# Two transformer blocks on one core: input sums on VectorE, modulation pairs in other places, gates head by head, one weight sum on GpSimd

## The chip, the cores and the metric

The kernel runs on one core of a Trainium2 chip. The time is that of the device, from the first to the last instruction and what lies around them, in microseconds (us). Lower is better. TensorE (PE) multiplies matrices, VectorE (DVE) and ScalarE (ACT) work on elements of SBUF and PSUM, GpSimd (POOL) works on SBUF alone, and SyncE (SP) issues the weight loads.

## The reference, cut to what matters

Two layers in a row on `x` of 512 tokens by 1024 features, all in fp32. The first has a gated spatial unit, forgetting attention and a SwiGLU feed-forward part:

```python
merged = jax.nn.sigmoid(g_a) * y_a + jax.nn.sigmoid(g_b) * y_b     # y_b: attention, y_a: spatial gating
x = x + rmsnorm(merged @ w_out[l], mix_post_g[l])
h = rmsnorm(x, ffn_pre_g[l])
x = x + rmsnorm(swiglu(h, w_gate[l], w_up[l], w_down[l]), ffn_post_g[l])
```

The second is a hybrid layer (short convolution, stick-breaking attention, a state-space mixer) whose norms are modulated by a vector `c`:

```python
mod = jax.nn.silu(c) @ mod_w + mod_b             # 1024 by 6144
shift1, scale1, gate1, shift2, scale2, gate2 = jnp.split(mod, 6, axis=-1)
h = rms_norm(x, g_pre_mix) * (1 + scale1) + shift1
merged = (sigmoid(gl_a) * y_a + sigmoid(gl_b) * y_b + sigmoid(gl_c) * y_c)
x = x + gate1 * rms_norm(merged @ w_o, g_post_mix)
h2 = rms_norm(x, g_pre_ffn) * (1 + scale2) + shift2
gt, up = jnp.split(h2 @ w_ffn_in, 2, axis=-1)
x = x + gate2 * rms_norm((silu(gt) * up) @ w_ffn_out, g_post_ffn)
```

## The kernel before

Every engine runs one program written out by hand, and the engines meet at semaphores; each engine works strictly in its own order. Every fp32 matrix product is made of three matmuls over a high and a low part of each operand: ACT casts a weight unit to its high part (`w_hi`, L1100), DVE subtracts to get the low part (`w_lo`, L1585, "split"), and PE multiplies high by high, high by low and low by high (L2295 to L2297). A weight unit is 1 MB, loaded by SP into one of two `raw` slots; a slot is free when the low part of the unit before in it is done.

**Seven-product units.** The up stage of both layers (`hidden` on DVE and ACT, `blocks` on POOL and PE) has 22 units. The first four (`tile`, `split`) are plain. The other 18 (`BLOCKS`) are multiplied as two-by-two blocks with seven products of 12 matmuls each instead of eight (`product`, L2389 to L2391, 256 columns), in the order p7 m, p6 m, p4 m, p1 m+1, p5 m, p2 m+1, p3 m. For this the inputs need four sums S1 to S4 of quarters of `h` (in `s_sum`, `s_hi`, `s_lo`), made once for each layer, and the weights four sums for each unit: t1 (DVE, L1729), t3 (DVE, L1735), t2 (POOL, L993), and t4 = t2 minus a quarter (POOL, L997). DVE then makes low parts: of the pair of raw quarters (`pair_lo`, L1742), of t3 and t2 (`sums_lo`, L1751, which waits for t4, since it overwrites what t4 reads), of t4 and t1 (L1758) and of the last quarter (`b22_lo`, L1765). DVE also adds the products: p2 (L1803), z (L1813), c21 (L1818), c22 (L1824), the gate multiplications (L1829, L1797). PE may begin p3 of a unit only when c22 of that unit is there. A step of this loop is called a turn here.

**The sums of the inputs.** At the start of the stage DVE makes S1 (L1770 to L1772) ahead of the first `tile`, POOL makes S3, S2 and S4 (L977 to L985).

**The modulation.** POOL makes `mod` in six pairs of 512 columns each times two: `mod_begin(pair)` clears `mod_acc` (L944), loads the bias and the first slab; `mod_step(pair, i)`, i = 0 to 15, issues the load of the next slab (L939, 256 KB), multiplies a slab by a scalar in each partition (L957) and adds it (L960). The 16th step raises `mod_summed`. A pair cannot begin before PE has read the one before (`mod_read`). Pairs 0 to 3 are turned to columns by eight transposes on PE (`mod_columns(pair)`, L2566), which wait for `mod_summed` of the pair, and summed by DVE (`mod_columns(pair, ...)`, L1700). Pairs 4 and 5 are gates (`mod_gate`, L2574). Pair 1 scales the norm ahead of the mixer of the second layer, pairs 2 (shift) and 3 (scale) belong to the norm ahead of its second feed-forward part.

| POOL makes | before | after |
|---|---|---|
| pair 0 | at the start | same |
| pair 1, steps | 8 before the layer norm's roots, 5 after, 3 in `blocks` of layer 1 | 9 before, 4 after, 3 in `blocks` (one each in turns 1 to 3) |
| pair 2 | `blocks` of layer 1, one step a turn | whole, in the down stage of layer 1 |
| pair 3 | whole, in the down stage of layer 1 | begins after the squares of the mixer's output in layer 2; two steps before `rr_ssm` (L1071), 14 after |
| pair 4 | after `rr_ssm` | after pair 3 |
| pair 5 | `blocks` of layer 2, one step a turn | 4 steps ahead of post-norm 2, 12 in `blocks` (turns 1 to 12) |

**The end of the mixer in layer 2.** PE runs gate unit n_mg, then the sums of squares (L2871), gate unit n_mg+1, the spread of the roots (L2877, which waits for DVE's `rr_diag`, which waits for POOL's `rr_ssm`), gate unit n_mg+2, then the branches' unit n_mg+3. A gate unit is 48 matmuls of 512 columns. After that come twelve more units, the output product `out2` (in it `mod_gate(4)`), post-norm 2 and the up stage of layer 2.

**The gates of the heads.** After the attention's last mask POOL adds 1 to the eight gate tiles (L1021), then multiplies the eight heads by them (L1024), then begins pair 1. The layer norm of the spatial unit needs POOL's roots (`ln_root`, L1031, L1032), which come after 8 steps of pair 1; DVE normalizes with them (L1945) and PE goes on with L2660.

Of the kernel before, what the change touches and what calls it, by code (L numbers as in the profile page):

```python
# [31 lines left out]
F32 = mybir.dt.float32  # L32
# [9 lines left out]
KD = D // P  # L42
# [101 lines left out]
def build(nc, a, out):  # L144
    with ExitStack() as ctx:
# [509 lines left out]
        def dve_order():  # L655


            yield from ("s1", "s1_lo", "s3_lo", "s24_lo", "t1 0", "t3 0", "pair 0", "sums 0", "t4 0", "t1_lo 0")
            for m in range(BLOCKS):
# [5 lines left out]
                yield from [f"t3 {ahead}"] if ahead else []  # L665
# [6 lines left out]
        def act_order():  # L672

            yield from ("s1_hi", "s3_hi", "s24_hi", "pair 0", "sums 0", "p1 0", "t4 0", "t1 0")
# [19 lines left out]
        def wait_pool(eng, which, m, total):  # L694


            eng.wait_ge(block_pool, (2 * BLOCKS + 3) * which + 2 * m + 3 + total)

        def wait_pool_sum(eng, which, done):


            eng.wait_ge(block_pool, (2 * BLOCKS + 3) * which + done)
# [178 lines left out]
        def _(gp):  # L881
# [91 lines left out]
            def blocks(n0, which, c):  # L973

                s1, s2, s4, s3 = (s_sum[:, i] for i in (S1, S2, S4, S3))
# [6 lines left out]
                wait_pool_sum(gp, which, 2)  # L982
                then(gp.tensor_tensor(s2, s2, h_quarter(h_lo, 0, 0), ALU.subtract))
                then(gp.tensor_tensor(s4, h_quarter(h_hi, 0, 1), s2, ALU.subtract))
                gp.tensor_tensor(s4, s4, h_quarter(h_lo, 0, 1), ALU.add).then_inc(block_pool, 1)  # L985
                if which == 0:
                    mod_step(1, 13)
                for m in range(BLOCKS):
                    n = n0 + PLAIN + m
                    t2, t4 = four(operand(w_sum, n0, 3)), four(t4_sum(n0, m))  # L990
# [1929 lines left out]
```

## Time and profile before

| | |
|---|---|
| median of 3 runs | 1578.08 us (1577.12 to 1578.24) |
| profiled execution, its own time | 1577.7 us |
| its span | 1576.0 us |
| granted TensorE clock, mean | 0.993 |
| busy: PE, DVE, POOL, ACT | 1533.7, 1018.0, 687.7, 669.8 us |
| idle of PE by waits | 35.6 us in 38 waits |

A busy PE is the sum over pipelined matmuls, so the waits of PE say more than its share. In a row of the timeline the text in brackets is how long the engine sat idle before the instruction, and what ended that.

### The profile page before, as it was taken

Reading aid. Unit: us, or ns where it says so; the run is one execution under the profiler, and the core shown is the slowest. Engines: PE = TensorE matmul, PEld = TensorE weight load, DVE = VectorE, ACT = ScalarE, POOL = GpSimd, SP = SyncE. Lnnn points to the kernel's source line nnn. Section 1 sums busy time; section 2 is a strip of 40 time slices with the busy share of each in tenths; the row PEclk is TensorE's granted clock in tenths of the full one; section 3 lists DMA queues with packets and bytes.
Section 4 is the critical chain, followed back from the end, with each engine's and each line's share of the span. In section 5 each row is a group of like instructions: output and inputs, shape, how many; then the busy total and the mean of one; then the engine's idle time right before and its main releaser. Section 6 shows DMA issues by size and latency. Waiting matters only on the chain.

```text
span 1576.0 us, 23248 instructions
## 1 busy us (share of the span) xinstructions
PE 1533.7 (97%) x8908; PEld 1346.1 (85%) x8908; DVE 1018.0 (65%) x1379; ACT 669.8 (43%) x1109; POOL 687.7 (44%) x543
## 2 busy tenths in 40 slices
PE   9999999979989999999999999999999899999998
PEld 9878788868889999988898888888889799999886
DVE  4342766447588999964276979643457799997423
ACT  6223444313454444442176775323236344544221
POOL 3871002760776656669120802691003666662000
PEclk9999999989999999999999999999999999999999
DMA  7532132422523434454322212443322243444231
GB/s 216 174 120 80 54 81 55 147 87 80 182 73 101 132 104 133 128 181 146 115 67 81 81 54 69 139 141 106 106 80 81 60 131 113 126 134 134 95 107 54
DMA packets 189620, 171.40 MB, mean 109 GB/s; under 512 B 20688, under 2 KB 162000, under 8 KB 189520
## 3 DMA queue, kind: packets, MB, share of 16 engines
q1 hardware_dynamic: 181456, 144.84, 30.6%
q0 software_dynamic: 8064, 25.20, 5.2%
q8 instruction: 67, 1.10, 0.3%
q14 instruction: 33, 0.27, 0.1%
HBM read 167.91 MB, written 2.10 MB: 108 GB/s over the span
## 4 chain that ended last, share of the span: by engine, by line
PE 70%; DVE 15%; POOL 9%; issue 4%; ACT 1%; DMA 0%; DVEq 0%; POOLq 0%; ACTq 0%
PE bank L2295 17%; PE bank L2297 17%; PE bank L2296 17%; POOL w_sum L997 3%; DVE w_lo L1751 3%; DVE act_m L1829 3%; POOL w_sum L993 2%; DVE w_lo L1742 2%; PE bank L2458 2%; PE bank L2459 2%; PE bank L2462 2%; DVE w_lo L1758 2%; DVE act_m L1729 1%; PE bank L2389 1%; PE bank L2616 1%
## 5 line engine op out<-in xcount | busy, mean ns | idle before, releaser
L1585 DVE TENSOR_TENSOR w_lo<-raw,w_hi 128x2048 fp32r<-128x2048 f32 (+1 forms) x109 | 216.3, 1985 | 239.4 <-ACT w_hi L1100 239.3
L2295 PE MATMUL bank<-h_hi,w_hi 128*128 128x512 f32 (+1 forms) x800 | 310.9, 389 | 11.1 <-DVE w_lo L1585 11.1
L2297 PE MATMUL bank<-h_hi,w_lo 128*128 128x512 f32 (+1 forms) x800 | 299.8, 375 | 0.0
L2296 PE MATMUL bank<-h_lo,w_hi 128*128 128x512 f32 (+1 forms) x800 | 299.6, 375 | 0.0
L1100 ACT CAST w_hi<-raw 128x2048 fp32r<-128x2048 f32 (+1 forms) x108 | 171.4, 1587 | 199.4 <-PE bank L2297 191.8
L957 POOL TENSOR_SCALAR mod_raw<-mod_raw,c_silu 128x512 f32<-128x512 f32 x96 | 197.0, 2053 | 19.3 <-DMA mod_raw<-in_mod_w 15.6
L2295 PEld LDWEIGHTS bank<-h_hi,w_hi 128*128 128x128 f32 x800 | 151.9, 190 | 40.0 <-DVE w_lo L1585 12.4
L2389 PE MATMUL bank<-s_hi,w_hi 128*128 128x256 f32 x576 | 166.7, 289 | 13.4 <-DVE act_m L1824 13.4
L2296 PEld LDWEIGHTS bank<-h_lo,w_hi 128*128 128x128 f32 x800 | 152.0, 190 | 27.4 <-issue 1.9
L2297 PEld LDWEIGHTS bank<-h_hi,w_lo 128*128 128x128 f32 x800 | 151.6, 189 | 27.7
L2391 PE MATMUL bank<-s_hi,w_lo 128*128 128x256 f32 x576 | 162.9, 283 | 0.0
L2390 PE MATMUL bank<-s_lo,w_hi 128*128 128x256 f32 x576 | 162.9, 283 | 0.0
L960 POOL TENSOR_TENSOR mod_acc<-mod_acc,mod_raw 128x512 f32<-128x512 f32 x96 | 138.1, 1438 | 8.3
L2389 PEld LDWEIGHTS bank<-s_hi,w_hi 128*128 128x128 f32 x576 | 110.2, 191 | 20.0 <-DVE act_m L1824 19.9
L2389 PE MATMUL bank<-h_hi,w_hi 128*128 128x256 f32 x432 | 122.4, 283 | 0.0
L2390 PE MATMUL bank<-h_lo,w_hi 128*128 128x256 f32 x432 | 122.2, 283 | 0.0
L2391 PE MATMUL bank<-h_hi,w_lo 128*128 128x256 f32 x432 | 122.1, 283 | 0.0
L2390 PEld LDWEIGHTS bank<-s_lo,w_hi 128*128 128x128 f32 x576 | 110.3, 192 | 0.0
L2391 PEld LDWEIGHTS bank<-s_hi,w_lo 128*128 128x128 f32 x576 | 110.3, 192 | 0.0
L2295 PE MATMUL bank<-w_hi,act_hi 128*128 128x512 f32 x280 | 109.0, 389 | 0.0
L2297 PE MATMUL bank<-w_hi,act_lo 128*128 128x512 f32 x280 | 108.9, 389 | 0.0
L2296 PE MATMUL bank<-w_lo,act_hi 128*128 128x512 f32 x280 | 108.9, 389 | 0.0
(476 smaller groups left out, 3348.3 us busy)
## 6 DMA issues: line engine op xcount, KB each, us to landing
raw<-in_w_in SPq DMA_DIRECT2D x102, 512.0 KB, 4.5
mod_raw<-in_mod_w POOLq DMA_DIRECT2D x96, 256.0 KB, 3.0
raw<-in_w_ffn_in SPq DMA_DIRECT2D x44, 512.0 KB, 4.9
raw<-in_w_gate SPq DMA_DIRECT2D x22, 512.0 KB, 4.0
raw<-in_w_up SPq DMA_DIRECT2D x22, 512.0 KB, 5.3
raw<-in_w_down SPq DMA_DIRECT2D x20, 512.0 KB, 4.5
raw<-in_w_ffn_out SPq DMA_DIRECT2D x20, 512.0 KB, 4.5
raw<-in_w_out SPq DMA_DIRECT2D x8, 512.0 KB, 4.3
```

The source lines that it names most:

```text
L957: then(gp.tensor_scalar(mod_raw[:, s, :], mod_raw[:, s, :], c_silu[:, k:k + 1], None, ALU.mult))
L960: ins = gp.tensor_tensor(acc, acc, mod_raw[:, s, :], ALU.add)
L997: gp.tensor_tensor(t4, t2, quarter_of(n, 1, 0), ALU.subtract).then_inc(block_pool, 1)
L1100: ins = act.copy(w_hi[s][:, cols], raw[s][:, cols])
L1585: ins = dve.tensor_tensor(w_lo[s][:, cols], raw[s][:, cols], w_hi[s][:, cols].bitcast(F32), ALU.subtract)
L1751: dve.tensor_tensor(operand_pair(w_lo, n0, 2), operand_pair(w_sum, n0, 2), operand_pair(w_hi, n0, 2).bitcast(F32), ALU.subtract).then_inc( ...
L2295: pe.matmul(o, st_hi, mv_hi, start=first, stop=False)
L2296: pe.matmul(o, st_hi, mv_lo, start=False, stop=False)
L2297: return pe.matmul(o, st_lo, mv_hi, start=False, stop=last)
L2389: pe.matmul(o, hi[:, k, :], mv_hi(k), start=first and k == 0, stop=False, skip_group_check=not first)
L2390: pe.matmul(o, hi[:, k, :], mv_lo(k), start=False, stop=False, skip_group_check=not first)
L2391: ins = pe.matmul(o, lo[:, k, :], mv_hi(k), start=False, stop=k == 3, skip_group_check=not first)
```

## The change

The input sums S1, S2 and S4 are all made by DVE, later than before (S1 after the first tile and the first split, S2 and S4 after t1 of block 0); POOL makes S3 alone, and waits ahead of its last part for the low part of unit 2. t3 is made by POOL, ahead of t2, instead of DVE. The pairs of the modulation move as in the table above; PE's transposes of pair 1 go to the last block of layer 1, those of pair 2 to the down stage, and those of pair 3 stand ahead of the branches' first unit, where PE waits for `mod_summed` of that pair; DVE's sums of the columns move with them. The low and high parts of hidden tiles 4 and 5 move from turn 8 to the first unit of the down stage. The gates are added to and applied head by head in one loop.

```diff
             def blocks(...)        # POOL
-                wait_dve(gp, which, "s1")
-                gp.tensor_tensor(s2, s1, h_quarter(h_hi, 0, 0), ALU.subtract).then_inc(block_pool, 1)
-                then(gp.tensor_tensor(s2, s2, h_quarter(h_lo, 0, 0), ALU.subtract))
-                then(gp.tensor_tensor(s4, h_quarter(h_hi, 0, 1), s2, ALU.subtract))
-                gp.tensor_tensor(s4, s4, h_quarter(h_lo, 0, 1), ALU.add).then_inc(block_pool, 1)
+                gp.wait_ge(lo_done, n0 + 3)      # ahead of the last part of s3
                 for m in range(BLOCKS):
+                    wait_operand_free(gp, n0, which, m, 2)
+                    gp.tensor_tensor(t3, quarter_of(n, 1, 1), quarter_of(n, 0, 1), ALU.subtract).then_inc(block_pool, 1)
                     wait_dve(gp, which, f"t1 {m}")
...
-                    if which == 0:
-                        if m == 0:
-                            mod_step(1, 14)
-                            mod_step(1, 15)
-                        elif m == 1:
-                            mod_begin(2)
-                        else:
-                            mod_step(2, m - 2)
-                    elif m == 0:
-                        mod_begin(5)
-                    elif m <= 2 * KD:
-                        mod_step(5, m - 1)
+                    if 1 <= m <= 2 * KD - done:
+                        mod_step(pair, done + m - 1)
...
             for f in range(KD):
                 wait_emptied(gp, n_g + 4 + f // 2, f % 2)
                 then(gp.tensor_scalar(gates[:, KD + f, :], gates[:, KD + f, :], 1.0, None, ALU.add))
-            for f in range(KD):
                 gp.wait_ge(head_out, f + 1)
                 gp.tensor_tensor(q_t[:, f, :], q_t[:, f, :], gates[:, KD + f, :], ALU.mult).then_inc(gated_b, 1)
             mod_begin(1)
-            for i in range(8):
+            for i in range(9):
                 mod_step(1, i)
...
-            blocks(n_up, 0, 1)
-            mod_pair(3)
+            blocks(n_up, 0, 1, 1, 13)
+            mod_pair(2)
...
+            mod_begin(3)
+            for i in range(2):
+                mod_step(3, i)
             gp.wait_ge(ms2_ready, 1)
             gp.tensor_tensor(rr_ssm[:], ms_ssm[:], ...).then_inc(rr_ready, 1)
+            for i in range(2, 2 * KD):
+                mod_step(3, i)
             mod_pair(4)
             mod_lo_part(4)
+            mod_begin(5)
+            for i in range(4):
+                mod_step(5, i)
             post_norm(2)
-            blocks(n_up2, 1, 3)
+            blocks(n_up2, 1, 3, 5, 4)
...
             # DVE, start of hidden
+                tile(n0, 0, 0)
+                split(n0 + 2)
                 dve.wait_ge(h_lo_done, 2 * KD * (c + 1))
                 then(dve.tensor_tensor(s1, h_quarter(h_hi, 1, 0), h_quarter(h_hi, 1, 1), ALU.add))
...
+                then(dve.tensor_tensor(s2, s1, h_quarter(h_hi, 0, 0), ALU.subtract))
+                then(dve.tensor_tensor(s2, s2, h_quarter(h_lo, 0, 0), ALU.subtract))
+                then(dve.tensor_tensor(s4, h_quarter(h_hi, 0, 1), s2, ALU.subtract))
+                dve.tensor_tensor(s4, s4, h_quarter(h_lo, 0, 1), ALU.add).then_inc(block_dve, 1)
...
             # DVE, in a turn
-                    if m + 1 < BLOCKS:
-                        t3_part(m + 1)
-                    if m == 2 and which == 0:
-                        mod_columns(1, gain_3, True)
-                    if m == 8:
-                        hidden_lo(which, PLAIN)
-                        hidden_lo(which, PLAIN + 1)
...
             # PE
             pe.wait_ge(ssm_lo_done, 4)
-            pe.wait_ge(mod_out, 4)
-            branches(n_mg + 3, STILL)
+            mod_columns(3)
+            branches(n_mg + 3, STILL, 4)
```

## Rows read from the trace of the kernel before

**Rows 1.** Waits of PE: engine, line, releaser: us in total, times, longest.

```profile
PE bank L2389 <- DVE act_m L1824: 13.4, 32, 1.3
PE bank L2295 <- DVE w_lo L1585: 11.1, 2, 6.6
PE bank L2660 <- DVE v_sgu L1945: 9.0, 1, 9.0
```

**Rows 2.** Chain that ended last, by time (start us, us, what), PE at the mixer's end.

```profile
1000.42 1.78 PE bank L2877 x16
1002.20 0.23 PE bank L2295
```

**Rows 3.** Timeline of ACT: start us, us, line, operation; idle before in brackets.

```profile
1013.14 0.60 ACT L1190 ACTIVATE sig<-bank 128x512 f32<-128x512 f32 x1 [3.94 <-PE bank L2297]
```

**Rows 4.** Timeline of POOL from the squares on, pair 4's first steps and fifteenth.

```profile
979.37 3.21 POOL L1069 TENSOR_TENSOR z_t<-z_t 128x512 f32<-128x512 f32 x1
990.92 1.68 POOL L1071 TENSOR_TENSOR rr_ssm<-ms_ssm,power 128x8 f32<-128x8 f32 x1 [8.34 <-DVE ms_ssm L2238]
992.55 0.96 POOL L944 MEMSET mod_acc<- 128x1024 f32 x1
...
1000.31 1.57 POOL L957 TENSOR_SCALAR mod_raw<-mod_raw,c_silu 128x512 f32<-128x512 f32 x1 [4.30 <-DMA mod_raw<-in_mod_w]
1004.19 2.65 POOL L957 TENSOR_SCALAR mod_raw<-mod_raw,c_silu 128x512 f32<-128x512 f32 x1
...
1058.29 1.58 POOL L957 TENSOR_SCALAR mod_raw<-mod_raw,c_silu 128x512 f32<-128x512 f32 x1
```

**Rows 5.** Timeline of DVE, the diagonals of the roots.

```profile
994.09 1.65 DVE L2242 TENSOR_SCALAR rr_diag<-ident,rr_ssm 128x128 f32<-128x128 f32 x8
```

**Rows 6.** Stretches around PE's longest wait; the column after POOL is the granted clock.

```profile
340.00:345.00 5.00, 0.00 (x1) 0.00 (x1) 3.25 (x4) 0.00 (x0) 3.58 (x7) 0.50 0.00 0
345.00:350.00 5.00, 5.00 (x22) 4.72 (x23) 2.68 (x4) 0.00 (x0) 0.00 (x0) 0.60 0.00 0
```

**Rows 7.** Timelines, POOL's heads' gates and pair 1, then DVE's layer norm.

```profile
284.35 14.14 POOL L1024 TENSOR_TENSOR q_t<-q_t,gate_a 128x512 f32<-128x512 f32 x8
304.18 1.57 POOL L957 TENSOR_SCALAR mod_raw<-mod_raw,c_silu 128x512 f32<-128x512 f32 x1 [2.33 <-DMA mod_raw<-in_mod_w]
...
286.14 0.69 DVE L1898 COPY q_t<-bank 128x512 f32<-128x512 f32 x1 [3.30 <-PE bank L2639]
340.07 0.81 DVE L1945 TENSOR_SCALAR v_sgu<-v_sgu,mean_var,inv_rms 128x1024 f32<-128x1024 f32 x1 [9.74 <-POOL inv_rms L1032]
```

**Rows 8.** Timeline of POOL and DVE in one turn.

```profile
557.11 1.29 POOL L993 TENSOR_TENSOR w_sum<-raw,act_m 128x512 f32<-128x512 f32 x1 [3.42 <-DVE act_m L1729]
557.24 1.72 DVE L1735 TENSOR_TENSOR w_sum<-raw 128x512 f32<-128x512 f32 x1
558.55 1.56 POOL L997 TENSOR_TENSOR w_sum<-w_sum,raw 128x512 f32<-128x512 f32 x1
```

**Rows 9.** Chain that ended last, in turns with a step and around turns 2 and 8.

```profile
520.75 1.21 DVE mod_sum L1700 x2
...
552.53 1.44 DVE act_m L1829
...
563.14 1.43 DVE act_m L1829
...
585.79 1.21 DVE act_lo L1710 x2
```

**Rows 10.** Timeline of DVE, start of the up stage in layer 1.

```profile
457.79 3.67 DVE L1585 TENSOR_TENSOR w_lo<-raw,w_hi 128x2048 fp32r<-128x2048 f32 x1 [1.11 <-ACT w_hi L1100]
496.72 0.42 DVE L1824 TENSOR_TENSOR act_m<-bank,act_m 128x256 f32<-128x256 f32 x1
```

**Rows 11.** Timeline of POOL at post-norm 2; and PE's gate product, first and last start.

```profile
1186.19 0.32 POOL L894 TENSOR_SCALAR sq_y<-sq_y 128x1 f32<-128x1 f32 x1 [23.77 <-ACT y_out L1106]
L2574 PE MATMUL bank<-mod_lo,ones_r x4: 389/389/389, 1165.5 to 1487.4; 128*128 128x512 f32 x4
```

More of the change, by code:

```diff
@@ L655, in dve_order @@
         def dve_order():
-            yield from ("s1", "s1_lo", "s3_lo", "s24_lo", "t1 0", "t3 0", "pair 0", "sums 0", "t4 0", "t1_lo 0")
+            yield from ("s1", "s3_lo", "t1 0", "s24", "s1_lo", "pair 0", "s24_lo", "sums 0", "t4 0", "t1_lo 0")
             for m in range(BLOCKS):
@@ L672, in act_order @@
         def act_order():
-            yield from ("s1_hi", "s3_hi", "s24_hi", "pair 0", "sums 0", "p1 0", "t4 0", "t1 0")
+            yield from ("s3_hi", "s1_hi", "pair 0", "s24_hi", "sums 0", "p1 0", "t4 0", "t1 0")
             for m in range(BLOCKS):
@@ L694, in wait_pool @@
         def wait_pool(eng, which, m, total):
-            eng.wait_ge(block_pool, (2 * BLOCKS + 3) * which + 2 * m + 3 + total)
-        def wait_pool_sum(eng, which, done):
-            eng.wait_ge(block_pool, (2 * BLOCKS + 3) * which + done)
+            eng.wait_ge(block_pool, (3 * BLOCKS + 1) * which + 3 * m + 1 + total)
         POST_UNIT = [n_out + 3, n_dn + 11, n_out2 + 3, n_dn2 + 11]
@@ L971, in mod_pair, with blocks @@
                     mod_step(pair, i)
-            def blocks(n0, which, c):
-                s1, s2, s4, s3 = (s_sum[:, i] for i in (S1, S2, S4, S3))
+            def blocks(n0, which, c, pair, done):
+                s3 = s_sum[:, S3]
                 gp.wait_ge(h_lo_done, 2 * KD * (c + 1))
@@ L1033, in _ @@
             gp.wait_ge(merged, KD)
-            for i in range(8, 13):
+            for i in range(9, 13):
                 mod_step(1, i)
             post_norm(0)
-            blocks(n_up, 0, 1)
-            mod_pair(3)
+            blocks(n_up, 0, 1, 1, 13)
+            mod_pair(2)
             post_norm(1)
@@ L1144, in post_norm @@
                 for j in range(units):
-                    if units == 6 and 1 <= j <= 4:
-                        for t in range(4 * j + 2, 4 * j + 6):
+                    if units == 6 and j <= 4:
+                        for t in range(4 if j == 0 else 4 * j + 2, 4 * j + 6):
                             hidden_hi(k // 2, t)
@@ L1225, in t4_t1_hi @@
                 def t4_t1_hi(m):
-                    wait_pool(act, which, m, 2)
+                    wait_pool(act, which, m, 3)
                     wait_operand_free(act, n0, which, m, 4)
@@ L1638, in post_norm @@
                 for j in range(units):
-                    if units == 6 and 1 <= j <= 4:
-                        for t in range(4 * j + 2, 4 * j + 6):
+                    if units == 6 and j <= 4:
+                        for t in range(4 if j == 0 else 4 * j + 2, 4 * j + 6):
                             hidden_lo(k // 2, t)
@@ L1784, in hidden @@
                                   ALU.subtract).then_inc(block_dve, 1)
-                t1_part(0)
-                tile(n0 + 2, 2, 0)
-                t3_part(0)
-                pair_lo(0)
                 sums_lo(0)
@@ L2437, in blocks @@
                     product(m, 6, "x", *sums(S4), first=False)
-                    if m == 0 and which == 0:
-                        mod_columns(1)
             def token_unit(n, x_hi, x_lo, k0, first, last, pace, width=512, tiles=range(NT)):
@@ L2848, in gate_unit, with branches @@
                     feature_tile(n, f, pace)
-            def branches(n, pace):
+            def branches(n, pace, columns=0):
                 u = UNITS[n]
@@ L2857, in branches @@
                     wait(pe, emptied[2 + f], u["round"] + pace.by(pace.rounds))
+                    if f == 1:
+                        wait(pe, mod_out, columns)
                     for b, k0, x_hi, x_lo, kt in ((4 + 2 * f, 2, sb_hi, sb_lo, 2), (5 + 2 * f, 4, ssm_hi, ssm_lo, 4), (2 + f, 0, sc_hi, sc_lo, 2)):
```

62 lines of the change are left out of this document (25 added, 37 removed).

## The prediction

> **What bounds the kernel now.** I read the waits of PE first. There are only three that matter [rows 1]: 13.4 us before p3 of 32 turns, on c22 of DVE; 11.1 us in two waits for a low part, at the start of the two up stages; 9.0 us for the layer norm of the spatial unit. Elsewhere PE never stops for long, so a change pays only by shortening these three, and it costs wherever it makes PE stop anew. Then I read the timelines of POOL and DVE around each place that the change touches, to see how much earlier than PE's need each moved piece is ready.
>
> **Part 1, pair 3 moved to the end of the mixer.** This is the largest term. PE spreads the roots at 1000.42 and starts gate unit n_mg+2 at 1002.20 [rows 2]. ACT takes that unit's second tile at 1013.14 [rows 3], so PE is at the branches' unit n_mg+3 at 1013.1. In the new program it first has to transpose pair 3 there, and for that POOL must have done all 16 steps.
>
> When can POOL have done them? The squares end at 979.37 + 3.21 = 982.6 [rows 4]. The moved `mod_begin` issues three loads after its memset; for pair 4 the first multiplication came 1000.31 - 992.55 = 7.8 us after the memset [rows 4], so for pair 3 it starts at about 990.4, or some 2 us sooner if the first slab lands sooner. A step is 3.88 us at best (1004.19 - 1000.31) and 4.14 us on the mean of fourteen (1058.29 - 1000.31 = 57.98), which ran beside DVE's work [rows 4]. The two steps ahead of `rr_ssm` take 7.8 to 8.3 us, to 996.2 to 998.7. Only then does POOL make `rr_ssm`, which it did at 990.92 before, after an idle time of 8.34 us. It ends at about 998.5 (997 to 1000), and DVE's diagonals (1.65 us, [rows 5]) end at 1000.2 instead of 995.7. PE wants them at 1000.42: the cover of nearly 5 us is used up, and I take 0 to 1.5 us of wait, 0.5 in the sum.
>
> Fourteen steps are left. At 3.88 they are 54.3 us, at 4.14 58.0. DVE has little to do once PE stands, so I take 56.5: the last sum is there at 998.5 + 56.5 = 1055.0. PE stands from 1013.1 to 1055.0, 41.9 us (the 0.5 of above is inside this). Ends: 997 + 54.3 = 1051.3, 38 us; 1000 + 58 + 1 = 1059, 46 us. Nothing covers this wait: on PE's queue all that follows stands behind the transposes, and SP's loads, ACT and DVE wait for PE in turn. The eight transposes themselves only change place.
>
> After so long an idle time PE starts slowly. In the one long wait of now the granted clock was 0.50 in the stretch of the wait and 0.60 in the next 5 us [rows 6], that is the lower of the two levels, 1.2 GHz, for four of these five, after which it is at 2.4 GHz. Working through 4 us at half speed costs 2.0 us. Part 1 in all: **+44** (40 to 49).
>
> **Part 2, what stands behind it.** Pair 4 takes POOL 78 us more, to about 1134, while PE, shifted by 44, wants it at 1165.5 + 44 = 1209 [rows 11]: covered by 75 us. Pair 5 begins only when PE has read pair 4, about 1 us after that. Seen in the old times: 1166.5, first step 7.8 us later, four steps to 1190 (1187 at best), where POOL's first root was due at 1186.19 [rows 11]. POOL's root of tile 0 is thus 1 to 4 us late. DVE multiplies a second bank before it uses this root, which covers about 2 us. I take +0.5 (0 to 3).
>
> **Part 3, the gates head by head.** POOL's eight multiplications began at 284.35, when the last gate tile was done, and took 14.14 us [rows 7]. Seven of the heads are there long before; head 7 is copied at 286.14 [rows 7]. One multiplication is left after it: end at about 289.5 instead of 298.5. Pair 1 begins 9 us earlier, and has 9 steps instead of 8 before the roots, one more of about 4.2 us. The roots come 4.8 us earlier. They are what DVE's normalization waited 9.74 us for [rows 7], and PE's wait of 9.0 us hangs on that. The gain is 4.8 (2 to 8), and with the shorter idle time perhaps a little of the slow clock: **-5**. The seven multiplications now lie beside the attention, whose DVE steps mostly read PSUM; I take nothing for that, and 1 us if they get in its way.
>
> **Part 4, the start of the up stages.** PE waits 11.1 us in two waits [rows 1] for the split that stands behind S1 on DVE (457.79, 3.67 us, [rows 10]). With the tile and split first, the split neither waits for S1 nor runs beside a sum of POOL, and PE's wait nearly goes. But DVE has not less to do in the stage's start: it gains three sums of 1.1 us, each beside POOL's t3, t2 and t4. Laying out DVE's new order by its durations, I come to the first c22 at about 496, where it was at 496.72 [rows 10]; PE meets the wait later, in small pieces. So I take **-2** for both stages (0 from the layout, up to -10 if all of PE's earlier start is kept, +2 if POOL's t3 delays S2 and S4 more).
>
> **Part 5, the turns.** A turn with a step of the modulation takes 563.14 - 552.53 = 10.61 us [rows 9]. PE has 84 matmuls in it, which is 10.1 us when the mean wait of 13.4/32 = 0.42 [rows 1] and 0.1 for starting again are taken off. The loop that sets the 10.61 runs over DVE and POOL: pair_lo, b22_lo, t1, then POOL's t2 and t4, then sums_lo, c22, the low parts of t4 and t1, the gate. Three edits change it:
> - t3 leaves DVE, where it took 1.72 us beside t2 [rows 8], but stood off the loop: DVE waits for t4 after it anyway. t4 becomes 1.29 instead of 1.56 [rows 8], and starts a little sooner: -0.33.
> - t3 on POOL (about 1.29, as t2 in [rows 8]) can start only after p7, which is about when DVE ends pair_lo. Then it holds up b22_lo, and with it t1 and t2: +0.8.
> - Without a step of the modulation, DVE's gate multiplication (1.44 us in [rows 9]) is 0.41, and t1's low part is freer: -1.25.
>
> A turn with a step becomes 10.61 - 0.33 + 0.8 = 11.1, a turn without one 10.61 - 0.33 - 1.25 + 0.8 = 9.8 by DVE and POOL. Then PE's own loop counts (p3, p7, t3, b22_lo, t1, t2, t4, sums_lo, c22), which I add up to 10.25, so it is 10.25 (10.08 to 10.4). Layer 1 has 3 turns with a step and 13 without: 3 x 0.5 - 13 x 0.35 = -3.1, and turns 2 and 8 lose their extra 1.21 us each [rows 9], -2.4; in all -5.5. Layer 2 has 12 with and 4 without: 12 x 0.5 - 4 x 0.35 = +4.6, less 1.2 of turn 8: +3.4. Together **-2** (-9 to +6). The columns' sums and the tiles 4 and 5 moved to the down stage stand there ahead of splits that PE needs over 1 us later: nothing.
>
> *A rule weighed.* DVE's t3 starts at 557.24 and ends 0.56 us after POOL's t2 (558.40), so it waited for it and needs 0.56 us itself [rows 8]. If every such pair shut each other out, a turn could not be shorter than the sum: on DVE 4.8 us (two of 1024 columns, four of 512, one of 256, at 0.56 for 512), on POOL 6.7 us in a turn with a step (four of 1.29, one of 1.57 [rows 4]), together 11.5 instead of my 11.1. The same sum for the kernel of now, with t3 on DVE, is 10.8, where 10.61 is measured [rows 9]. The Trainium skill states this exclusion (SBUF — State Buffer, section "SBUF: two separate sides"): the pair of ports goes to whichever of the two engines starts first, for the whole instruction. The rows of t3 agree, the length of a turn does not quite; by the rule 15 turns would cost 6 us more.
>
> **Sum.** 44 + 0.5 - 5 - 2 - 2 = +35.5 to the profiled execution's 1577.7 us gives 1613.2; that execution stands 0.4 us under the median, so the runs' median should be **1614** us.
>
> **Rivals.**
> - *The stall does not come* (PE's need for pair 3 is covered after all). Then 1577.7 - 8.5 = 1569. It decides at one point: the 16 steps would have to be over by 1013.1. For it speaks only that the mixer's part has idle time of POOL (8.34 us before `rr_ssm`). Against it: 14 steps at 3.88 us after 998. It is faster than before: chance 0.03. If POOL's steps ran in half the time, the stall would be 15 us and the result 1587: 0.04.
> - *The stall comes, and the other parts give more*: PE keeps its earlier start in both up stages, all turns without a step run at 10.1, and the roots come 8 us earlier: -8 - 4 - 3 further, 1600. Chance 0.13.
> - *The stall is longer and t3 hurts more*: steps at 4.14 us throughout and the first slab late, +4, the up stages give nothing, +2, the turns with a step take 11.4, +4.5: 10.5 more, 1624. Chance 0.13.
> - *Full exclusion in the turns with a step*: 15 turns at 11.5 instead of 11.1, +6, 1620. For it speaks t3's row, against it that it gives 10.8 for the 10.61 of now. Chance 0.07. The page named above states it.
> - *The forecast*, 1605 to 1622 in all its small terms: chance 0.60.
>
> The range is 1602 to 1624. A measurement of this kernel tells 0.2%, 3.2 us, from no change. Faster by more than that 0.03, the same 0.01, slower 0.96.
>
> **What the profile of the changed kernel would show.** Right: one wait of PE of 38 to 46 us before the transposes of pair 3, released by POOL's last `mod_acc`; a granted clock near 0.5 in it and a little after; 14 steps of 3.9 to 4.1 us in it on POOL; the wait at L2660 near 4 to 5 us; the wait for a low part at the start of the up stages under 1 us each, but others after it; turns of about 10.25 without and 11.1 with a step. Wrong: if pair 3's steps end before PE is there, part 1 falls, and with it the sign. If the turns with a step stay at 10.6, POOL's t3 found a gap that I do not see. If the first c22 of the stage comes at 491 instead of 496, part 4 was too small by 5 us for each stage.

## The result, and the profile after

The changed kernel takes 1613.73 us (median of 4 runs, 1611.45 to 1614.3) where the kernel before, timed beside it, takes 1577.63 us: a ratio of 1.0226, 95% interval 1.0208 to 1.0244. The profiled execution took 1614.3 us, its span 1612.6 us, 36.6 more than the 1576.0 of before. The forecast was 1614.

The waits of PE in the changed kernel (columns as in [rows 1]):

```profile
PE bank L2535 <- POOL mod_acc L954: 37.6, 1, 37.6
PE bank L2362 <- DVE act_m L1801: 13.0, 20, 1.1
PE bank L2629 <- DVE v_sgu L1916: 6.6, 1, 6.6
PE bank L2362 <- DVE w_lo L1718: 3.4, 2, 1.7
PE bank L2848 <- DVE rr_diag L2214: 3.1, 1, 3.1
```

One row is new and longer than all waits of before together (35.6 us): the transposes of pair 3 (L2535) stand 37.6 us for POOL's last `mod_acc`. The 11.1 us for the low part at the start of the up stages ([rows 1], second row) are gone, the spatial unit waits 6.6 instead of 9.0 us, and the diagonals of `rr_ssm`, which cost PE nothing before, 3.1 us.

The same place on POOL, from the first step of pair 3 on, and on PE (timelines):

```profile
979.34 2.27 POOL L951 TENSOR_SCALAR mod_raw<-mod_raw,c_silu 128x512 f32<-128x512 f32 x1 [3.19 <-DMA mod_raw<-in_mod_w]
981.70 1.28 POOL L954 TENSOR_TENSOR mod_acc<-mod_acc,mod_raw 128x512 f32<-128x512 f32 x1
983.28 0.58 POOL L933 DMA_DIRECT2D mod_raw<-in_mod_w  x1 [0.30 <-POOL mod_acc L954]
983.90 2.66 POOL L951 TENSOR_SCALAR mod_raw<-mod_raw,c_silu 128x512 f32<-128x512 f32 x1
...
988.01 1.68 POOL L1053 TENSOR_TENSOR rr_ssm<-ms_ssm,power 128x8 f32<-128x8 f32 x1
989.66 0.63 POOL L933 DMA_DIRECT2D mod_raw<-in_mod_w  x1
990.33 1.67 POOL L951 TENSOR_SCALAR mod_raw<-mod_raw,c_silu 128x512 f32<-128x512 f32 x1
...
1044.44 1.26 POOL L954 TENSOR_TENSOR mod_acc<-mod_acc,mod_raw 128x512 f32<-128x512 f32 x1
1045.85 1.51 PE L2535 MATMUL bank<-ident,mod_acc 128*128 128x128 f32 x6 [37.58 <-POOL mod_acc L954]
```

POOL has no gap over 0.30 us between 988.01 and 1045.70: `rr_ssm`, then fourteen steps in 56.0 us (989.66 to 1045.70), 4.0 each. PE starts 0.15 us after the last of them.

The windows around the end of that wait (columns as in [rows 6]; the granted clock stands after POOL):

```profile
1008.00:1045.00 37.00, 0.27 (x2) 0.00 (x0) 2.29 (x1) 2.38 (x2) 33.33 (x28) 0.54 0.32 92
1045.00:1050.00 5.00, 4.15 (x14) 3.70 (x15) 1.45 (x3) 0.00 (x0) 2.50 (x4) 0.50 0.00 0
1050.00:1055.00 5.00, 5.00 (x19) 4.00 (x19) 0.00 (x0) 0.00 (x0) 2.81 (x4) 0.82 0.34 106
1055.00:1060.00 5.00, 5.00 (x24) 4.13 (x23) 3.44 (x5) 0.62 (x1) 4.49 (x5) 1.00 0.20 52
```

PE works from 1045.85 on, at 0.50 (1.2 GHz) until nearly 1052, then at 2.4 GHz.

**Where the 36.6 us arose.** I took the start of the same instruction in both traces and subtracted (after minus before, running total):

| place | before | after | total | own share |
|---|---|---|---|---|
| PE, spatial unit (L2660, L2629) | 345.00 | 343.07 | -1.9 | gates, -1.9 |
| PE, second transposes of the norm ahead of the up stage, layer 1 | 441.76 | 440.55 | -1.2 | within what single runs differ by |
| DVE, first c22, layer 1 | 496.72 | 494.04 | -2.7 | start of the stage, -1.5 |
| DVE, c22 of turn 16, layer 1 | 669.05 | 659.20 | -9.8 | turns, -7.2 |
| PE, transposes behind the down stage | 796.33 | 786.48 | -9.8 | 0 |
| DVE, first merge after the mixer | 1018.68 | 1055.31 | +36.6 | pair 3, +46.5 |
| PE, second transposes of post-norm 2 | 1210.16 | 1247.31 | +37.1 | +0.5 |
| DVE, first c22, layer 2 | 1267.70 | 1300.82 | +33.1 | start of the stage, -4.0 |
| DVE, c22 of turn 16, layer 2 | 1438.52 | 1475.12 | +36.6 | turns, +3.5 |

Between the first two rows the total changes by +0.7: the stretch takes 97.48 us at a mean granted clock of 0.97, where it took 96.76 at 0.98 (windows 343.07:440.55 and 345.00:441.76). The first row belongs to this one execution of the changed kernel. Eight of the experiments below (e1 to e4, e7 to e10) run the same program up to there, and PE waits 4.7 to 4.9 us in them, not 6.6; part 3 below comes back to this.

### The profile page after: what moved, and what is told of

It is laid out like the page before. It is cut to its first block, busy times and chain, and to the rows that moved or that the text cites. A ratio compares the mean times of both kernels' runs of the same rounds, so it can differ in the third digit from the quotient of the medians.

```text
span 1612.6 us, 23286 instructions
## 1 busy us (share of the span) xinstructions
PE 1535.8 (95%) x8908; PEld 1347.0 (84%) x8908; DVE 970.4 (60%) x1351; ACT 669.0 (41%) x1109; POOL 710.6 (44%) x571
## 4 chain that ended last, share of the span: by engine, by line
PE 71%; DVE 11%; POOL 11%; issue 4%; ACT 2%; DMA 1%; DVEq 0%; SPq 0%; POOLq 0%; ACTq 0%
PE bank L2268 15%; PE bank L2270 15%; PE bank L2269 15%; PE bank L2362 4%; PE bank L2364 4%; PE bank L2363 4%; POOL mod_raw L951 3%; POOL mod_acc L954 2%; PE bank L2430 2%; PE bank L2429 2%; PE bank L2433 2%; DVE w_lo L1727 2%; POOL w_sum L987 1%; POOL w_sum L983 1%; DVE w_lo L1718 1%
## 5 line engine op out<-in xcount | busy, mean ns | idle before, releaser
L1568 DVE TENSOR_TENSOR w_lo<-raw,w_hi 128x2048 fp32r<-128x2048 f32 (+1 forms) x109 | 212.6, 1951 | 231.9 <-ACT w_hi L1087 231.7
L951 POOL TENSOR_SCALAR mod_raw<-mod_raw,c_silu 128x512 f32<-128x512 f32 x96 | 192.2, 2002 | 22.8 <-DMA mod_raw<-in_mod_w 19.0
L980 POOL TENSOR_TENSOR w_sum<-raw 128x512 f32<-128x512 f32 x36 | 64.8, 1800 | 141.1 <-PE bank L2364 125.2
```

What stands on the lines that cost most here:

```text
L951: then(gp.tensor_scalar(mod_raw[:, s, :], mod_raw[:, s, :], c_silu[:, k:k + 1], None, ALU.mult))
L980: gp.tensor_tensor(t3, quarter_of(n, 1, 1), quarter_of(n, 0, 1), ALU.subtract).then_inc(block_pool, 1)
L1568: ins = dve.tensor_tensor(w_lo[s][:, cols], raw[s][:, cols], w_hi[s][:, cols].bitcast(F32), ALU.subtract)
```

## The experiments

All twelve were timed beside the kernel before; the ratio is to that one, and where two experiments come from different series they are compared by their ratios.

**e1_two_steps and e2_eight_steps: is it the wait?** Steps of pair 3 left out behind `rr_ssm` (the loads of their slabs go with them).

```diff
-            for i in range(2, 2 * KD):
+            for i in (14, 15):                       # e1
+            for i in (2, 3, 4, 5, 6, 7, 14, 15):     # e2
                 mod_step(3, i)
```

> Left out: 12 of the 14 steps of pair 3 that stand behind rr_ssm (steps 2 to 13), so the sum of this pair is incomplete. Theory (the added time is the time that PE stands before the transposes of pair 3): the two steps that stay behind the root end at about 993 + 8 = 1001, PE is there only at about 1010, so its wait of 37.6 us goes and with it the slow clock after it (2 to 3 us): 1614 - 40 = 1573 to 1574 us. Rival (the pair's work costs by lying beside DVE and PE, or the rest of the change costs, and PE's wait would be filled by another): the time stays over 1590 us, with a new wait of PE in the trace after 1010.

> Left out: steps 8 to 13 of pair 3, so the sum of this pair is incomplete; eight of the fourteen steps behind rr_ssm stay. Theory (PE's wait is the time of the steps, one for one, and the slow clock behind it is a fixed sum): a step is 4.0 us, six fewer take 24 us off the wait of 37.6, which leaves 13.6, with the granted clock still at its lower level behind it: 1590 us. Rival (the wait isn't set by POOL's steps one by one, or the slow clock depends on the length of the wait): off this by more than 3 us.

e1: 1571.24 us, ratio 0.9953 (0.9937 to 0.9968). e2: 1589.14 us, 1.0062 (1.0046 to 1.0078). PE's wait before the transposes is gone in e1; in e2 its timeline has

```profile
1021.59 1.94 PE L2541 MATMUL bank<-ident,mod_acc 128*128 128x128 f32 x8 [14.22 <-POOL mod_acc L960]
```

Six steps fewer shorten the wait by 23.4 us, 3.9 each, and the stretch from the down stage's transposes to the first c22 of layer 2 by 23.9 (the transposes themselves start 22.3 us earlier in it). Without a wait before the transposes (e1) that stretch is 41.0 us shorter than in the changed kernel: 37.6 of wait and 3.4 more, most of which is the low clock behind the wait (last section). The rival (another wait fills the gap) is out: e1 has no new one. It keeps the wait for the diagonals, 2.9 us, and behind it the clock is low as well (a window of e1, columns as in [rows 6]):

```profile
993.00:996.00 3.00, 3.00 (x13) 2.76 (x12) 3.00 (x5) 1.24 (x2) 2.92 (x2) 0.50 0.26 65
```

**e10_rr_first: is the 3.1 us wait for the diagonals a cost of its own?** `mod_begin(3)` stays, the two steps go behind the root.

```diff
             mod_begin(3)
-            for i in range(2):
-                mod_step(3, i)
             gp.wait_ge(ms2_ready, 1)
             gp.tensor_tensor(rr_ssm[:], ...)
...
+            for i in range(2):
+                mod_step(3, i)
             for i in range(2, 2 * KD):
                 mod_step(3, i)
```

> The changed kernel, with the two steps of pair 3 that stood ahead of rr_ssm put behind it. Theory (PE's two waits end in one, the time at which POOL's last step is done): rr_ssm comes about 5 us earlier, so the wait of 3.1 us for the diagonals goes, but POOL stands until 981.1 for its input and then takes 1.7 us for it, so the steps start 3.4 us later and the wait before the transposes grows by 3.1 + 3.4: 1614 + 3.4 = 1617 us. Rival (the 3.1 us wait for the diagonals is a cost of its own): 1611 us.

1613.31 us, ratio 1.0221 (1.0207 to 1.0235): no different from the changed kernel. The waits of PE:

```profile
PE bank L2535 <- POOL mod_acc L954: 43.8, 1, 43.8
PE bank L2362 <- DVE act_m L1801: 13.5, 20, 1.1
PE bank L2629 <- DVE v_sgu L1916: 4.7, 1, 4.7
```

The wait for the diagonals is gone and the one behind it has grown by 6.2 us. The time alone does not tell the two apart: the theory's 1617 us lies outside the interval of the ratio (1610.3 to 1614.7 us over the 1577.63 of the first series), the rival's 1611 just inside. The stretch does: from the down stage's transposes to the first merge behind the mixer it is 269.4 us, against 268.8 in the changed kernel, and the rival wants it 3.1 us shorter. So the 3.1 us cost nothing. Of the 3.4 us that the theory also expected, 1.2 came at the transposes. The steps start 4.1 us later (counted from the down stage's transposes), but `rr_ssm` (1.7 us) no longer stands among them, which the theory left out, and from the first multiplication to the last sum the sixteen steps took 63.4 us (981.88 to 1045.29) against 64.7 in the changed kernel (979.34 to 1045.70, less `rr_ssm`).

**e6_gates_apart and e11_six_before_roots: what do the gates and the ninth step do?**

```diff
             for f in range(KD):                      # e6
                 ...
                 then(gp.tensor_scalar(gates[:, KD + f, :], gates[:, KD + f, :], 1.0, None, ALU.add))
+            for f in range(KD):
                 gp.wait_ge(head_out, f + 1)
...
-            for i in range(9):                       # e11
+            for i in range(6):
                 mod_step(1, i)
             ...                                      # the roots
+            for i in range(6, 9):
+                mod_step(1, i)
             gp.wait_ge(merged, KD)
```

> The nine steps before the roots stay, but POOL adds 1 to all gate tiles first and multiplies only then. Theory: the eight multiplications take 14.1 us from 284.35, as before the change, and end at 298.5 instead of 290.7; all that follows on POOL is 7.8 us later, so PE's wait before the spatial unit grows from 6.6 to 14.4 us: 1614 + 7.8 = 1621 to 1622 us. Rival (the two orders are worth little, since what POOL does in the attention's stretch is slowed there): the time grows by under 3 us.

> The changed kernel with six instead of nine steps of pair 1 ahead of the spatial unit's roots; the other three follow right behind the roots. Theory (the roots wait for POOL's steps, and the gates' 7 to 8 us went into the ninth step and into longer steps): the roots are then bound by DVE's variance at 331, some 6 us earlier, PE's wait of 6.6 us goes and about 1 us of the slow clock behind it: 1606 to 1607 us. Rival (three steps beside DVE's later work make PE wait elsewhere): under 3 us gained.

e6: 1617.47 us, ratio 1.0254 (1.024 to 1.0268), 3.7 us above the changed kernel (4.4 by the ratios), half of what the theory said and more than the rival. POOL's first step starts 7.3 us later (304.37 instead of 297.06), near the 7.8 expected, but the nine steps take 37.1 us instead of 40.2, and PE waits 10.8 instead of 6.6 us:

```profile
PE bank L2630 <- DVE v_sgu L1917: 10.8, 1, 10.8
```

Why nine steps are longer in the changed kernel shows in its own timeline of POOL:

```profile
287.49 3.20 POOL L1003 TENSOR_TENSOR q_t<-q_t,gate_a 128x512 f32<-128x512 f32 x1 [2.78 <-DVE q_t L1869]
297.06 1.64 POOL L951 TENSOR_SCALAR mod_raw<-mod_raw,c_silu 128x512 f32<-128x512 f32 x1 [3.02 <-DMA mod_raw<-in_mod_w]
...
306.52 3.32 POOL L954 TENSOR_TENSOR mod_acc<-mod_acc,mod_raw 128x512 f32<-128x512 f32 x1
...
316.16 1.56 POOL L951 TENSOR_SCALAR mod_raw<-mod_raw,c_silu 128x512 f32<-128x512 f32 x1 [1.58 <-DMA mod_raw<-in_mod_w]
317.80 2.36 POOL L954 TENSOR_TENSOR mod_acc<-mod_acc,mod_raw 128x512 f32<-128x512 f32 x1
```

An addition of 1.29 us takes 3.32 or 2.36 here, beside DVE's splits, and a slab comes 1.6 us late. The late slab is this execution's alone: in the eight kernels with the same program up to there no slab is late, the nine steps take 38.1 to 38.9 us, and PE waits 4.7 to 4.9 us (4.7 in the list of e10 above). Against these e6 makes the wait 6 us longer. e11: 1607.24 us, ratio 1.018 (1.0166 to 1.0193), 6.5 to 7.3 below the changed kernel, as the theory said. PE does not wait for the spatial unit (0.1 us is left), but its timeline a little later has

```profile
353.54 0.50 PE L2270 MATMUL bank<-h_hi,w_hi 128*128 128x512 f32 x1 [2.19 <-DVE w_lo L1570]
```

PE starts the spatial unit 6.5 us earlier than in the changed kernel (336.61 instead of 343.07), and then finds a low part 2.2 us away. The granted clock is 1.00 from there to the norm's transposes, where it was 0.97 over 97 us; the 2.2 us use up most of what this gives back. So the roots were late by POOL's steps alone: they now wait for DVE's variance.

**e3_no_steps_turns, e4_t3_dve and e5_before_t3_pool: what sets a turn?** e3 leaves out steps 4 to 13 of pair 5; e4 gives t3 back to DVE; e5 is the kernel before with t3 on POOL.

```diff
+                    if which == 1 and m in (12, 13):      # e3
+                        mod_step(5, m + 2)
-                    if 1 <= m <= 2 * KD - done:
+                    if which == 0 and 1 <= m <= 2 * KD - done:
                         mod_step(pair, done + m - 1)
...
-                    gp.tensor_tensor(t3, quarter_of(n, 1, 1), quarter_of(n, 0, 1), ...)      # e4; e5 adds it
+                    dve.tensor_tensor(t3, quarter_of(n, 1, 1), quarter_of(n, 0, 1), ...)     # behind z; e5 takes it away
```

> Left out: steps 4 to 13 of pair 5, so the sum of this pair is incomplete; turns 2 to 11 and one more of layer 2's up stage have no step of the modulation, turns 12 and 13 keep one each. Theory (a turn with a step is 11.07 us by the loop over DVE and POOL, a turn without one 10.11 by PE): ten turns fewer with a step give 10 x 0.96 = 9.6 us: 1604 us. Rival (the turns of layer 2 are long for another cause than the steps, such as t3 on POOL by itself): they stay near 11 and the time near 1614.

> t3 is back on VectorE in both layers (ahead of the turn's pair_lo, as before the change), all else as in the changed kernel. Theory (t3 on POOL lengthens the loop over DVE and POOL by holding up b22_lo, and this loop sets only the turns with a step of the modulation): those turns go from 11.07 to 10.6 us, the turns without one stay at 10.1, where PE's own work sets them. Fifteen turns with a step (12 in layer 2, 3 in layer 1): 15 x 0.46 = 6.9 us less, 1607 us. Rival (t3 has no part in the longer turns, the new order on DVE has): 1614 us.

> The kernel before with t3 moved to POOL and nothing else. Theory: its 30 turns with a step go from 10.61 to 11.07 us, since POOL's t3 comes ahead of t2 and holds up b22_lo: 30 x 0.46 = 13.8 us more, 1591 to 1592 us. Rival (t3 costs the same on either engine, and the 11.07 come from another part of the change): 1578 us.

e3: 1602.53 us, ratio 1.0154 (1.0139 to 1.017). e4: 1602.74 us, 1.0148 (1.0132 to 1.0163). e5: 1596.14 us, 1.0106 (1.0093 to 1.012). From c22 to c22 in the traces:

| | turn with a step | turn without | sixteen turns, layer 1 | layer 2 |
|---|---|---|---|---|
| before | 10.60 | 10.11 (one) | 172.33 | 170.82 |
| changed | 11.07 | 10.11 | 165.16 | 174.30 |
| e3 | 11.05 (layer 1) | 10.11 | 164.94 | 164.54 |
| e4 | 10.60 | 10.08 | 162.14 | 166.80 |
| e5 | 11.06 | - | 180.31 | 179.07 |

The four combinations of t3's engine and step or no step give 11.07, 10.60, 10.11 and 10.08: t3 on POOL costs 0.47 us where a step of the modulation stands in the turn, and 0.03 where none does. The rivals of e3, e4 and e5 are out. e4 gains more than the 6.9 us named (10.5 in the turns), since behind the last turn with a step the loop has to catch up: the three turns there take 9.45 to 10.13 us with t3 on DVE and 10.18 to 10.86 with t3 on POOL. e5 loses more than 13.8 (16.2 in the turns), 1 us in each turn 8 and 2.3 in the two starts of the stage. This is how t3 acts; first a turn of the changed kernel on DVE and POOL, then one of e4:

```profile
1337.61 1.23 DVE L1718 TENSOR_TENSOR w_lo<-raw,w_hi 128x1024 fp32r<-128x1024 f32 x1
1339.09 1.45 DVE L1741 TENSOR_TENSOR w_lo<-raw,w_hi 128x512 fp32r<-128x512 f32 x1
1340.47 0.68 DVE L1712 TENSOR_TENSOR act_m<-raw 128x512 f32<-128x512 f32 x1
...
1337.90 2.10 POOL L980 TENSOR_TENSOR w_sum<-raw 128x512 f32<-128x512 f32 x1 [0.84 <-PE bank L2364]
1341.22 1.29 POOL L983 TENSOR_TENSOR w_sum<-raw,act_m 128x512 f32<-128x512 f32 x1 [1.23 <-DVE act_m L1712]
```

```profile
1331.27 1.21 DVE L1737 TENSOR_TENSOR w_lo<-raw,w_hi 128x1024 fp32r<-128x1024 f32 x1
1332.74 0.68 DVE L1760 TENSOR_TENSOR w_lo<-raw,w_hi 128x512 fp32r<-128x512 f32 x1
1333.34 0.68 DVE L1722 TENSOR_TENSOR act_m<-raw 128x512 f32<-128x512 f32 x1
...
1334.15 1.29 POOL L991 TENSOR_TENSOR w_sum<-raw,act_m 128x512 f32<-128x512 f32 x1 [3.42 <-DVE act_m L1722]
```

From `pair_lo` to t1 it is 2.86 us with t3 on POOL and 2.07 without. t3 is issued at 1337.90, is shut out by `pair_lo` until 1338.8, runs its 1.3 us to 1340.0, and in that time DVE's `b22_lo` (L1741) is shut out in turn: 1.45 us instead of 0.68. Of the 0.79 lost, 0.3 comes back: t4 takes 1.30 us on POOL instead of 1.56.

The start of the up stages, from the second transposes to the first c22, comes out of the same runs:

| | layer 1 | layer 2 |
|---|---|---|
| old order of the sums, t3 on DVE (before) | 54.96 | 57.54 |
| old order, t3 on POOL (e5) | 56.42 | 58.37 |
| new order, t3 on DVE (e4) | 53.10 | 53.18 |
| new order, t3 on POOL (changed) | 53.49 | 53.51 |

The new order is worth 1.9 and 4.4 us (2.9 and 4.9 with t3 on POOL), and t3 on POOL takes 0.3 to 1.5 of it back.

**e7_pair3_early, e8_early_t3_dve_2, e9_pair5_late, e12_best: the same work elsewhere.** They leave nothing out. The cut is shortened, and what stands in words is several lines of the same kind; DVE's sums of the columns and PE's transposes of pairs 1 and 2 move with their pairs too.

```diff
-            gp.wait_ge(merged, KD)                   # e7
-            for i in range(9, 13):
+            for i in range(9, 16):
                 mod_step(1, i)
+            mod_begin(2), steps 0 to 3 of pair 2
             post_norm(0)
-            blocks(n_up, 0, 1, 1, 13)
-            mod_pair(2)
+            blocks(n_up, 0, 1, 1, 16)
+            steps 4 to 15 of pair 2, mod_begin(3), steps 0 to 11 of pair 3
             post_norm(1)
+            steps 12 to 15 of pair 3                 # and none at the mixer's end
...
-            mod_columns(3)                           # PE, ahead of the branches: moved behind unit n_v2
...
             # e8: e7, and t3 on DVE in layer 2
-            blocks(n_up2, 1, 3, 5, 4)                # e9: e8, t3 on DVE in both layers, and
+            blocks(n_up2, 1, 3, 5, 16)
+            steps 4 to 15 of pair 5
             mod_lo_part(5)
             # e12: e9, and six steps of pair 1 before the roots, ten behind them
```

> Nothing is left out; the steps stand elsewhere: pair 1's last seven and four of pair 2 in the stretch in which POOL has 50 us of idle time (342 to 392), the rest of pair 2 and twelve steps of pair 3 in the down stage of layer 1, four of pair 3 behind post-norm 1; none in the turns of layer 1 and none at the mixer's end. Theory (the change loses by PE's wait for pair 3 alone): all of part 1 goes, 46.5 us with the slow clock and the wait for rr_ssm, and three turns of layer 1 lose their step, 3 x 1.0 us: 1614 - 49.5 = 1564 to 1565 us, below the kernel before (1578) by 13 us. Rival (POOL's steps make post-norm 0, post-norm 1 or the down stage late instead): new waits of PE there, and over 1570 us.

> The kernel with pair 3 made early (1568.3 us), and t3 back on VectorE in layer 2, where twelve turns have a step of the modulation. Theory: 12 x 0.46 = 5.5 us less, 1562 to 1563 us. Rival (t3 has no part in the longer turns): 1568 us.

> Nothing is left out. The kernel with pair 3 early and t3 on VectorE (now in both layers), and pair 5's last twelve steps moved out of layer 2's turns into its down stage, with the copy, the low part and PE's spread of this pair one or three units later there. Theory (the turns with a step are set by the loop over DVE and POOL, those without by PE): twelve turns go from 10.60 to 10.08 us, 6.2 us less than the 1562.9 of the kernel with t3 on VectorE in layer 2: 1556 to 1557 us. Rival (twelve steps take 47 us in the down stage and PE's spread of pair 5 at about 1477 has to wait): a new wait of PE there, over 1562 us.

> Pair 3 early, t3 on VectorE in both layers, pair 5's twelve steps in the down stage of layer 2, and six instead of nine steps of pair 1 ahead of the spatial unit's roots. Nothing is left out. Theory (the parts are independent): 1556.5 from the kernel without the last edit, less its wait of about 4.8 us and 1 us of slow clock: 1551 us, 27 us below the kernel before. Rival (ten steps of pair 1 and four of pair 2 behind the roots delay post-norm 0): 1556 us or more.

| | us | ratio to before (95%) |
|---|---|---|
| e7 | 1568.30 | 0.9941 (0.9928 to 0.9955) |
| e8 | 1562.94 | 0.9901 (0.9887 to 0.9914) |
| e9 | 1555.60 | 0.9853 (0.9840 to 0.9867) |
| e12 | 1551.24 | 0.9826 (0.9813 to 0.9839) |

All beat both kernels; e12 by 28 us the kernel before and by 62 the changed one. e8, e9 and e12 came out as their theory said, within 0.4 us. e7 came out 3.5 us above it, for a part of the rival's reason: POOL has eleven steps behind the roots, and from the spatial unit to the second transposes of the norm ahead of the up stage e7 takes 100.2 us, where the kernels without these steps take 96.4 to 97.8. PE's timeline has a wait there that the changed kernel has not:

```profile
372.85 0.50 PE L2271 MATMUL bank<-h_hi,w_hi 128*128 128x512 f32 x1 [1.31 <-DVE w_lo L1571]
```

e12 pays this too (101.1 us). Another 2.4 us lie between the transposes behind the down stage and the first merge behind the mixer, where e7 is 44.1 us shorter instead of the 46.5 of part 1. The 1.0 us of pair 3's transposes still stands there, and PE has two new waits of 0.4 and 0.3 us; the rest is not traced. The spatial unit's wait, 4.9 instead of 6.6 us, gives 1.7 back. Of e12, the waits of PE:

```profile
PE bank L2295 <- DVE w_lo L1583: 3.0, 2, 2.8
PE bank L2389 <- DVE w_lo L1742: 2.4, 2, 1.2
PE bank L2389 <- DVE act_m L1828: 2.2, 4, 0.6
PE bank L2389 <- ACT act_m L1275: 2.2, 2, 1.1
```

PE's wait on c22, 13.4 us in [rows 1], is down to 2.2; the three great waits of before are gone, and the turns (10.08 us) are PE's own work.

## Why the prediction was right

The steps are those of the prediction, in its order.

**Part 1, forecast +44 (40 to 49): +46.5.** The mechanism and nearly every size hold. In times of before (the changed kernel is 9.86 us ahead there): the two steps and `rr_ssm` end at 999.5 (forecast 998.5), the fourteen steps take 56.0 (56.5), the last sum is there at 1055.6 (1055.0), and PE begins its transposes at 1055.7. The unit behind them it begins in the timelines (before, then changed) at

```profile
1012.94 0.39 PE L2295 MATMUL bank<-sb_hi,w_hi 128*128 128x512 f32 x1
1047.44 0.78 PE L2268 MATMUL bank<-sb_hi,w_hi 128*128 128x512 f32 x1
```

So PE comes to its transposes 42.8 us late (forecast 41.9). In it are the waits of 3.1 and 37.6 us and the low clock behind the first. The rest of the 46.5 lies behind the wait. First, the transposes were booked as "only change place": true for the whole kernel, since the 1.04 us (L2566) are gone from layer 1, but here they are an addition, and at the low clock they put the unit off by 1.6. Second, the clock stays low until 6.0 us after the wait, not 4, and the unit takes 2.1 us longer. The total is 42.8 + 1.6 + 2.1. That the wait for the diagonals is 3.1 and not 0.5 changes nothing, as the prediction had it, and as e10 shows; e1 and e2 show that the rest is the wait, step by step.

**Part 2, forecast +0.5 (0 to 3): +0.5.** POOL's first root comes at 1225.57, 2.8 us behind its place of before (1186.19 + 36.6), within the 1 to 4 us forecast, and no wait of PE there is over 0.3 us. In the eleven other kernels that have these four steps there (all but e5) the stretch is 0 to 0.3 us longer than before, so the 0.5 is no firm number.

**Part 3, forecast -5 (2 to 8): -1.9 in this execution, about -4 in the others.** With the late slab, the last multiplication's start and the first root are 49.7 us apart; in the eight other kernels they are 48.1 apart, and PE's wait is 4.1 to 4.3 us shorter than the 9.0 of before. Direction and size hold there, but by two errors that cancel. The head-by-head order was to bring 9 us, and brings 6 (10.8 us of wait in e6, 4.7 to 4.9 with the loop); the ninth step was to take 4.2 back, and takes 1.8 (10.8 in e6, 9.0 before, which has eight steps in the same order). The last multiplication takes 3.20 us beside DVE's splits and ends at 290.7 (forecast 289.5), the first step follows 6.4 instead of 5.7 us behind it, and nine steps that begin earlier meet more of DVE's work: 38.1 to 38.9 us, against 37.1 in e6. The term that was mis-sized is thus that one more step costs the mean of a step. The "little of the slow clock" was not given back (0.97 against 0.98). e11 shows that three steps fewer take the whole wait away.

**Part 4, forecast -2 for both: -5.5.** -1.5 in layer 1, -4.0 in layer 2. The range reached to -10; the value taken came from a layout of DVE's order. The first c22 came at 494.0, or about 495 in times of before (the stage starts 1.2 us earlier), where 496 was forecast. The size was missed, and the 2x2 table above gives its parts: t3's own cost in the start is small in the new order (0.3 to 0.4 us), and the order alone is worth 1.9 and 4.4 us. The layout had no term for the clock, and its rows changed most (windows of the two starts, before and then changed):

```profile
441.76:496.72 54.96, 50.52 (x322) 45.87 (x320) 45.12 (x40) 23.60 (x35) 40.30 (x19) 0.97 0.32 86
1210.16:1267.70 57.54, 50.91 (x322) 46.23 (x320) 46.18 (x44) 26.48 (x40) 32.27 (x17) 0.94 0.28 78
440.55:494.04 53.49, 49.83 (x322) 44.72 (x320) 40.22 (x41) 23.87 (x35) 19.00 (x11) 1.00 0.29 77
1247.31:1300.82 53.51, 49.84 (x322) 44.74 (x320) 43.50 (x46) 26.94 (x40) 19.00 (x11) 1.00 0.28 77
```

The waits of 4.4 and 6.6 us for the low part had a low clock behind them; the new waits in each start add up to 3.7 us, none over 1.7, and the clock is never low. How much of the 5.5 us is the clock, no run separates.

**Part 5, forecast -2: -3.7.** A turn with a step 11.07 (11.1), one without 10.11 (10.25), each as forecast to 0.15 us. Layer 1 -7.2 (forecast -5.5; up to 1.0 of the difference are the transposes booked in part 1), layer 2 +3.5 (+3.4). The working holds in its terms too: 0.79 for the time that t3 takes from `b22_lo` (0.8), 0.3 back at t4 (0.33), and 10.60 + 0.47 = 11.07 by e4 and e5.

**The rule weighed.** The turn is 11.07 where full exclusion would give 11.5, and 10.60 with t3 on DVE where it would give 10.8. Single pairs do shut each other out: t3 and `pair_lo` above. POOL's multiplication by a scalar, issued at 1333.46 in the same turn, takes 2.17 instead of 1.57, as it would if it waited for the low part that DVE has under way (L1727, to 1334.19). But then it runs on beside DVE's next ones, also of two tensors in SBUF:

```profile
1333.46 2.17 POOL L951 TENSOR_SCALAR mod_raw<-mod_raw,c_silu 128x512 f32<-128x512 f32 x1
1334.45 0.84 DVE L1734 TENSOR_TENSOR w_lo<-w_sum,w_hi 128x512 fp32r<-128x512 f32 x1
```

The low part takes 0.84 instead of 0.68 us and ends before the multiplication does, in 13 of the 15 turns with a step. In the other two it meets POOL's addition and takes 1.46. The Trainium skill (SBUF — State Buffer, section "SBUF: two separate sides") states that the pair of ports goes to one engine for a whole instruction when DVE reads two tensors of SBUF and GpSimd reads SBUF too. The rows of t3 and of the addition bear this out, those of the multiplication do not; as a sum over a turn the rule is too strict, and the trace decides.

**The rivals.** None took place. "No stall" was priced at 1569, and e1, which makes it come true, gives 1571.24; the half-length stall was priced at 1587 with 15 us, and e2, with 14.2, gives 1589.14. "The other parts give more" (priced at 1600; its own terms, 15 us under 1613.2, give 1598) had a part of its way: up stages and turns gave 5.2 us more than forecast, the roots 3.1 less (about 1 less in the other kernels), and part 1 cost 2.5 more. The sum 46.5 + 0.5 - 1.9 + 0.7 - 5.5 - 3.7 is 36.6; that it lies so near the forecast's 35.5 owes something to errors that cancel.

## What to carry to other kernels

Work that is spread over an idle engine may be nearly free in one place and cost 46 us in another: what counts is when its consumer comes, so for each moved piece write down when its inputs allow it, how long it takes and when the consumer wants it, and move it towards idle time ahead of that (here pair 3 into the down stage, pair 5 out of the turns). Where two waits of an engine hang on one chain of another, only the last counts; removing the first moves its time into the second. A small term read off one execution (the 1.9 us of part 3) can be a late load of that execution: the same stretch in kernels that share the code tells. And a two-engine loop is priced by which instruction stands between two that must follow each other, not by the sum of either engine: t3 costs the same 1.3 us on POOL in every turn, but 0.47 in a turn only where the loop, and not PE, sets the pace.

## What the runs showed of the hardware

The eight diagonals of DVE (a multiplication of one tensor by a scalar in each partition, 128x128) took 1.65 us alone [rows 5] and 3.90 beside POOL's step (timeline of DVE, changed kernel):

```profile
982.15 2.98 DVE L1568 TENSOR_TENSOR w_lo<-raw,w_hi 128x2048 fp32r<-128x2048 f32 x1 [0.81 <-ACT w_hi L1087]
989.72 3.90 DVE L2214 TENSOR_SCALAR rr_diag<-ident,rr_ssm 128x128 f32<-128x128 f32 x8 [4.59 <-POOL rr_ssm L1053]
993.55 2.28 DVE L1568 TENSOR_TENSOR w_lo<-raw,w_hi 128x2048 fp32r<-128x2048 f32 x1
```

In e10 they took 3.42 us beside a step. So an operation of DVE with one tensor at its input can lose as much as one with two. The Trainium skill (SBUF — State Buffer, section "SBUF: two separate sides") counts DVE's two-port modes among the cases that lock the pair; that these diagonals run in one, no row here tells. The split above it can be followed from both sides: it begins at 982.15 while POOL's addition runs to 982.98, takes 2.98 instead of 2.28 and ends at 985.13; POOL's multiplication, begun at 983.90, ends at 986.56, which is 1.43 after the split. The cost went to whichever came second. It was harmless here, as the diagonals hid inside the longer wait.

The granted clock stayed low for 6.0 us of work after 37.6 us of standing, and for 3.1 us after 14.2 us in e2 (windows of 1 us: 0.60 in 1051 to 1052 there, 0.64 in 1024 to 1025 here, and 1.00 behind both). Worked out from these, 1.94 - 1.04 on the transposes and half of the rest, it costs 3.0 and 1.5 us. From the start of the transposes to the first merge the three traces have 9.46, 8.17 and 6.63 us (changed, e2, e1), so against e1 it is 2.8 and 1.5: the two ways agree, and it is not "a fixed sum", as the expectation of e2 had it. The stretches less the waits say 3.4 and 2.9, but where a wait begins is known to a microsecond or so only (the same wait reads 36.1 to 37.8 us in five kernels in which the transposes start at the same place to 0.3 us). In e1 the clock fell after a wait of 2.9 us already (0.50 in the window 993 to 996).
